# A ring of four transposed inputs in the second mixer, and a last normalisation with its statistics on ScalarE

## What is computed

```python
def _s5_mixer(u, lam_re, lam_im, log_step, b_re, b_im, c_re, c_im, d_skip, w_glu, b_glu):
    ...
    for direction, reverse in ((0, False), (1, True)):
        ...
        bu = jnp.einsum('blgi,gpi->blgp', ugc, b_bar)
        _, states = lax.associative_scan(
            _diag_recurrence, (jnp.broadcast_to(lam_bar, bu.shape), bu), axis=1, reverse=reverse)
        ...
        y = y + jnp.real(jnp.einsum('blgp,gip->blgi', states, c_out))
    y = jax.nn.gelu(y.reshape(bsz, seqlen, S5_WIDTH))
    ...

def _layer_norm(x32, g, b):
    mu = jnp.mean(x32, axis=-1, keepdims=True)
    xc = x32 - mu
    var = jnp.mean(xc * xc, axis=-1, keepdims=True)
    return xc * lax.rsqrt(var + LN_EPS) * g.astype(jnp.float32) + b.astype(jnp.float32)
```

## Time and profile before

| | us |
|---|---|
| median of 3 runs | 3703.0 |
| lowest, highest | 3700.46, 3708.77 |
| the profiled execution | 3708.02 |
| its span, first to last instruction | 3706.2 |

### The profile page before, as it was taken

One profiled execution on the slowest core, in us unless ns is written; L12 is line 12 of the kernel. 1 busy time (PEld: TensorE's weight loads), 2 busy tenths in 40 slices (PEclk: granted clock), 3 DMA queues, 4 the chain that ended last, 5 costly groups with the idle time before them and its releaser, 6 DMA issues. The chain is left out here.

```text
span 3706.2 us, 33835 instructions
## 1 busy us (share of the span) xinstructions
PE 3153.6 (85%) x10424; PEld 1648.4 (44%) x10425; DVE 1432.8 (39%) x2033; ACT 540.3 (15%) x1058; POOL 1210.2 (33%) x1202
## 2 busy tenths in 40 slices
PE   7999999956787467759999928999999999999940
PEld 3555555532555344525555523444444444444420
DVE  2835423413788545513333361222122221222238
ACT  1112222211232100011111101101101101011012
POOL 0116766712666300002222202223222232222329
PEclk9999999977989777879999969999999999999975
DMA  5122232235222364262222124344454354442235
GB/s 238 74 76 80 99 118 94 82 137 211 66 82 89 94 183 145 77 239 91 97 97 91 53 119 151 102 136 125 130 163 126 113 154 152 117 121 45 56 95 206
DMA packets 131695, 437.62 MB, mean 118 GB/s; under 512 B 16884, under 2 KB 45300, under 8 KB 122644
## 3 DMA queue, kind: packets, MB, share of 16 engines
q1 hardware_dynamic: 86488, 291.18, 22.5%
q0 software_dynamic: 24752, 81.35, 9.2%
q10 hardware_dynamic: 20368, 63.94, 4.5%
HBM read 300.03 MB, written 136.38 MB: 118 GB/s over the span
## 5 line engine op out<-in xcount | busy, mean ns | idle before, releaser
L2008 PE MATMUL bank<-wg,exp_ht 128*128 x1008 | 455.0, 594 | 15.4 <-DVE exp_ht L2091 15.4
L2026 PE MATMUL bank<-wd,exp_hid_t 128*128 x1008 | 442.9, 592 | 0.9 <-ACT exp_hid_t L2062 0.9
L2008 PE MATMUL bank<-wu,exp_ht 128*128 x1008 | 442.9, 592 | 0.0
L1967 POOL DMA_INDIRECT x<-exp_out,exp_rows x63 | 102.6, 1629 | 870.0 <-DVE exp_out L2112 826.1
L2112 DVE TENSOR_TENSOR exp_out<-bank,exp_gates 128x512 f32<-128x512 f32 x126 | 81.2, 686 | 778.1 <-PE bank L2026 778.1
L1550 PE MATMUL bank<-mix_wo,mix_yt 128*128 128x512 f32 x768 | 342.4, 600 | 19.0 <-issue 11.5
L571 PE MATMUL bank<-x_t,w_in 128*128 128x512 f32 x768 | 336.0, 596 | 5.4 <-DVE x_t L481 5.4
L571 PE MATMUL bank<-w_in,x_t 128*128 128x264 f32 (+1 forms) x1152 | 339.6, 455 | 0.0
L2026 PEld LDWEIGHTS bank<-wd,exp_hid_t 128*128 128x128 f32 x1008 | 191.4, 190 | 241.6 <-issue 241.6
L2008 PEld LDWEIGHTS bank<-wu,exp_ht 128*128 128x128 f32 x1008 | 191.5, 190 | 241.1 <-issue 241.1
L2008 PEld LDWEIGHTS bank<-wg,exp_ht 128*128 128x128 f32 x1008 | 188.0, 192 | 227.5 <-issue 227.5
(11 more groups left out here) (350 smaller groups left out, 3830.2 us busy)
## 6 DMA issues: line engine op xcount, KB each, us to landing
wg<-in_w_gate SPq DMA_DIRECT2D x16, 2048.0 KB, 7.9
wu<-in_w_up SPq DMA_DIRECT2D x16, 2048.0 KB, 9.2
wd<-in_w_down SPq DMA_DIRECT2D x16, 2048.0 KB, 9.2
x_t<-in_x_t SPq DMA_DIRECT2D x6, 2048.0 KB, 9.2
mix_xt<-in_x SPq DMA_DIRECT2D x6, 2048.0 KB
x<-mix_v ACTq DMA_DIRECT2D x24, 512.0 KB, 2.6
h<-mix_h ACTq DMA_DIRECT2D x24, 512.0 KB, 2.7
com_v<-x SPq DMA_DIRECT2D x24, 512.0 KB, 3.9
```

Source lines behind the costliest of these rows:

```text
L1967: pool.indirect_dma_start(out=y_dram, out_offset=bass.IndirectOffsetOnAxis(ap=rows[:, j:j + 1], axis=0), in_=out[:, j, :], in_offset=None, ...
L2008: mul = pe.matmul(bank[:, :], ht[:, j, k, :], flat(of[:, bass.ds(e % 2, 1), k * DE:(k + 1) * DE]), start=k == 0, stop=k == KT - 1)
L2026: mul = pe.matmul(bank[:, :], hid_t[:, j, k, :], flat(wd[:, bass.ds(e % 2, 1), k * D + q * WIDE:k * D + (q + 1) * WIDE]), start=k == 0, st ...
```

## The change

In `s5_mixer`, `ut` gets four buffers (RING = 4). `turn_u(m)` waits for `y_mm` to reach m-3 instead of m-1, VectorE transposes pairs 0 and 1 first and then pair m+2 ahead of rotate(m). All else in that stage stays as it is.

`combine` is rewritten with six buffers. SyncE loads the first two tiles ahead of `ln_g` and `ln_b`. ScalarE sums each tile (Copy with an accumulated output), VectorE makes the negative mean of it (`centre`, 128x1), ScalarE sums the squares of the centred tile (Square with a bias and an accumulated output), GpSimd makes the reciprocal deviation in two 128x1 operations. VectorE then computes (v - mean) * `ln_g` (`scale`) and that times the reciprocal deviation plus `ln_b` (`shift`), each as one scalar-tensor-tensor operation. ScalarE issues the stores, three tiles behind its sums. In the diff the removed lines of `combine` are left out; they stand above.

```diff
@@ -1197,7 +1197,7 @@
 
     TC = T5 * CH5
     Q = (T5 + 1) * CH5
-    SLOTS = 3
+    SLOTS, RING = 3, 4
     GROUP = 32
     CG = C_ALL // GROUP
     PER = 20
@@ -1207,7 +1207,7 @@
         us = sb("us", [P, CG, HALF, 2, SSD])
         w, e = sb("w", [P, SLOTS, 2, HALF, 2, P]), sb("e", [P, SLOTS, 2, 2, Q])
         turn, toe = sb("turn", [P, SLOTS, 2, 2, C_ALL + 2]), sb("toe", [P, SLOTS, 2, HALF, TC])
-        ut = sb("ut", [P, 2, 2, HALF, C_ALL])
+        ut = sb("ut", [P, RING, 2, HALF, C_ALL])
         m1, m2, x = (sb(n, [P, 2, 2, C_ALL]) for n in ("m1", "m2", "x"))
         z, st = sb("z", [P, 2, 2, C_ALL]), sb("st", [P, 2, 2, 2, C_ALL])
         ys, yp = sb("ys", [C_S, T5, SSD]), sb("yp", [C_P, T5, SSD])
@@ -1251,9 +1251,9 @@
             @block.vector
             def _(dve):
                 def turn_u(m):
-                    j = m % 2
-                    if m >= 2:
-                        dve.wait_ge(y_mm, m - 1)
+                    j = m % RING
+                    if m >= RING:
+                        dve.wait_ge(y_mm, m - RING + 1)
                     for g in range(2):
                         at = (m * 2 + g) * CH5
                         dve.transpose(ut[:, j, g].rearrange("p k (a c) -> p a k c", c=GROUP),
@@ -1299,10 +1299,11 @@
                 dve.memset(z[:], 0.0).then_inc(cleared, 1)
                 dve.wait_ge(u_here, 128)
                 turn_u(0)
+                turn_u(1)
                 dve.wait_ge(cleared, 1)
                 for m in range(PAIRS):
-                    if m + 1 < PAIRS:
-                        turn_u(m + 1)
+                    if m + 2 < PAIRS:
+                        turn_u(m + 2)
                     rotate(m)
 
             @block.tensor
@@ -1318,7 +1319,7 @@
                             for k in range(HALF):
                                 for g in range(2):
                                     mul = pe.matmul(sums[j][d][g * N5:(g + 1) * N5, r * C_ALL:(r + 1) * C_ALL],
-                                                    w[:, s, r, k, d, g * N5:(g + 1) * N5], ut[:, j, g, k, :],
+                                                    w[:, s, r, k, d, g * N5:(g + 1) * N5], ut[:, m % RING, g, k, :],
                                                     start=k == 0, stop=k == HALF - 1)
                     mul.then_inc(states_mm, 1)
 
@@ -1332,7 +1333,7 @@
                         at, c = segments[n]
                         for k in range(HALF):
                             for g in range(2):
-                                pe.matmul(to[n][g], ut[:, j, g, k, at:at + c], toe[:, s, g, k, :], start=k == 0, stop=False)
+                                pe.matmul(to[n][g], ut[:, m % RING, g, k, at:at + c], toe[:, s, g, k, :], start=k == 0, stop=False)
                         if n == 0:
                             pe.wait_ge(e_here[s], loads(m))
                             pe.wait_ge(rotated, (m + 1) * PER)
@@ -2135,101 +2136,107 @@
 
 def combine(nc, C, S, y_dram, ln_g_row, ln_b_row, out_sample, out_prompt):
 
...
+    RING = 6
     with ExitStack() as ctx:
         sb = lambda n, s: ctx.enter_context(nc.sbuf_tensor("com_" + n, s, F32))
         ln_g, ln_b = sb("ln_g", [P, D]), sb("ln_b", [P, D])
...
+        v, y, unused = sb("v", [P, RING, D]), sb("y", [P, RING, D]), sb("unused", [P, 2, D])
+        total, minus, square, root = (sb(n, [P, RING]) for n in ("total", "minus", "square", "root"))
+        g_here, summed, centred, squared, rooted, scaled, shifted = (
+            S(n) for n in ("g_here", "summed", "centred", "squared", "rooted", "scaled", "shifted"))
         v_here, stored = ([S(f"{n}{r}") for r in range(RING)] for n in ("v_here", "stored"))
...
+        uses = lambda n: (n // RING + 1) * 16
+        one = lambda a, n: a[:, n % RING:n % RING + 1]
         with nc.Block() as block:
             @block.sync
             def _(sp):
...
                 for n in range(NT):
                     r = n % RING
                     if n >= RING:
...
+                        sp.wait_ge(scaled, n - RING + 1)
+                        sp.wait_ge(squared, n - RING + 1)
                     sp.dma_start(v[:, r, :], y_dram[n * P:(n + 1) * P, :]).then_inc(v_here[r], 16)
+                    if n == 1:
+                        sp.dma_start(ln_g[:], ln_g_row.to_broadcast([P, D])).then_inc(g_here, 16)
+                        sp.dma_start(ln_b[:], ln_b_row.to_broadcast([P, D])).then_inc(g_here, 16)
                 for r in range(RING):
...
+                    sp.wait_ge(stored[r], NT // RING * 16)
 
             @block.scalar
             def _(act):
...
+                def total_of(n):
+                    act.wait_ge(v_here[n % RING], uses(n))
+                    if n:
+                        act.wait_ge(summed, n)
                     if n >= RING:
...
+                        act.wait_ge(centred, n - RING + 1)
+                    act.activation(unused[:, 0, :], v[:, n % RING, :], ACT.Copy, accum_out=one(total, n)).then_inc(summed, 1)
+
+                def squares_of(n):
+                    act.wait_ge(centred, n + 1)
+                    if n:
+                        act.wait_ge(squared, n)
+                    if n >= RING:
+                        act.wait_ge(rooted, (n - RING) * 2 + 1)
+                    act.activation(unused[:, 1, :], v[:, n % RING, :], ACT.Square, bias=one(minus, n), accum_out=one(square, n)).then_inc(squared, 1)
 
                 def store(n):
...
                     act.wait_ge(shifted, n + 1)
                     to = out_sample[0, n * P:(n + 1) * P, :] if n < NT_SAMPLE else out_prompt[0, (n - NT_SAMPLE) * P:(n - NT_SAMPLE + 1) * P, :]
...
+                    act.dma_start(to, y[:, n % RING, :]).then_inc(stored[n % RING], 16)
+
+                total_of(0)
                 for n in range(NT):
...
+                    if n + 1 < NT:
+                        total_of(n + 1)
+                    squares_of(n)
                     if n >= 3:
                         store(n - 3)
                 for n in range(NT - 3, NT):
                     store(n)
+
+            @block.gpsimd
+            def _(pool):
+                for n in range(NT):
+                    pool.wait_ge(squared, n + 1)
+                    if n >= RING:
+                        pool.wait_ge(shifted, n - RING + 1)
+                    pool.tensor_scalar(one(root, n), one(square, n), 1.0 / D, EPS, ALU.mult, ALU.add).then_inc(rooted, 1)
+                    pool.wait_ge(rooted, n * 2 + 1)
+                    pool.tensor_tensor(one(root, n), one(root, n), C.minus_half[:], ALU.pow).then_inc(rooted, 1)
+
+            @block.vector
+            def _(dve):
+                def centre(n):
+                    dve.wait_ge(summed, n + 1)
+                    if n >= RING:
+                        dve.wait_ge(squared, n - RING + 1)
+                    dve.tensor_scalar(one(minus, n), one(total, n), -1.0 / D, None, ALU.mult).then_inc(centred, 1)
+
+                def scale(n):
+                    r = n % RING
+                    dve.wait_ge(centred, n + 1)
+                    if n >= RING:
+                        dve.wait_ge(stored[r], uses(n) - 16)
+                    dve.scalar_tensor_tensor(out=y[:, r, :], in0=v[:, r, :], scalar=one(minus, n), in1=ln_g[:],
+                                             op0=ALU.add, op1=ALU.mult).then_inc(scaled, 1)
+
+                def shift(n):
+                    r = n % RING
+                    dve.wait_ge(rooted, n * 2 + 2)
+                    dve.wait_ge(scaled, n + 1)
+                    dve.scalar_tensor_tensor(out=y[:, r, :], in0=y[:, r, :], scalar=one(root, n), in1=ln_b[:],
+                                             op0=ALU.mult, op1=ALU.add).then_inc(shifted, 1)
+
+                centre(0)
+                dve.wait_ge(g_here, 32)
+                for n in range(NT):
+                    if n + 1 < NT:
+                        centre(n + 1)
+                    scale(n)
+                    if n:
+                        shift(n - 1)
+                shift(NT - 1)
     S.clear()
```

More of the change, by code:

```diff
@@ L2136, in combine @@
 def combine(nc, C, S, y_dram, ln_g_row, ln_b_row, out_sample, out_prompt):
-    RING = 4
-    TURNS = NT // RING
+    RING = 6
     with ExitStack() as ctx:
@@ L2151, in _ @@
             def _(sp):
-                sp.dma_start(ln_g[:], ln_g_row.to_broadcast([P, D])).then_inc(g_here, 16)
-                sp.dma_start(ln_b[:], ln_b_row.to_broadcast([P, D])).then_inc(g_here, 16)
                 for n in range(NT):
@@ L2159, in _ @@
                 for r in range(RING):
[L2160 to L2166, removed]
-                    for q in range(2):
-                        dve.bn_stats(stats[:, r, q, :], v[:, r, q * WIDE:(q + 1) * WIDE]).then_inc(counted, 1)
-                    dve.wait_ge(counted, n * 2 + 2)
-                    dve.bn_aggr(mean[:, r, :], flat(stats[:, r:r + 1].rearrange("p a b c -> p (a b) c"))).then_inc(meant, 1)
-                def scale(n):
-                    r = n % RING
```

(45 more changed lines are left out.)

9 lines of the change are left out of this document (removed).

## The result

The changed kernel takes 3556.45 us (median of 4 runs, 3552.65 to 3561.33) against 3704.69 us for the kernel before (4 runs, 3700.46 to 3708.77; the three known ahead of the prediction and one more). The ratio is 0.9601, with a 95% interval of 0.9584 to 0.9617: 148 us less, where 139 were forecast.

The account below looks back on a forecast made before the run. Bounds: VectorE and TensorE taking turns in the second mixer, GpSimd's 4.48 us per tile in the last normalisation. 3708.0 - 102 - 36.7 = 3569.3, forecast as 3564 us because the median lies 5.0 lower; range 3550 to 3606.

Parts of the forecast that it names:

- The stall of the transposes goes: Second mixer: transposes for pair m+2 wait for output m-2 instead of m-1, so VectorE's 7.87 us stall goes.
- TensorE becomes the bound, at 9.45 us: Second mixer: TensorE's 9.45 us a pair exceeds VectorE's 9.13 by 0.3 us and sets the pace.
- The clock comes back in full: Second mixer: TensorE's granted clock, 0.80 over a pair before, returns to full level; 43 us of the gain hang on it.
- The beginning costs nothing: Second mixer's start: two more transposes (2 x 1.04 us) ahead of rotation 0 run beside TensorE's first states, at no cost.
- 1.7 us for one short wait in the middle: Middle of the second mixer: deduction of 1.7 us because the 3 MB store of the first half shares engines with loads.
- A tile of 3.0 us: Last normalisation: 3.0 us for each of 24 tiles, ends 2.82 and 3.42; stage gains 36.7 us, bounds 26.6 and 41.
- Start at `ln_g`'s landing: Last normalisation: VectorE's first scaling needs `ln_g` and starts at about 3592.0 again, though ScalarE can start up to 3.5 us earlier.
- A: Rival, second mixer: TensorE still falls to 1.2 GHz in each pair, mixer gains 60 us, total 3606; chance 0.09.
- D: Rival, second mixer: TensorE stays at 1.2 GHz throughout, 20.1 us a pair, total 3716, slower; chance 0.02.
- B: Rival, last normalisation: VectorE-GpSimd exchange becomes a chain of 4.5 us a tile, gaining nothing; total 3601, chance 0.08.
- C: Rival, second mixer: rotation waits for TensorE's states, pair stays at 17 us, only the normalisation gains; total 3666, chance 0.03.
- DMA as a possible bound: Last normalisation: DMA needs 2.69 us a tile; if ScalarE waits for loads of `v`, DMA was the bound.

Follow-up runs that it names:

- e9: Changed kernel without the second scalar-tensor-tensor operation of each tile and with each store of the last normalisation writing half the columns; one run, 3544.28 us.
- e8: Changed kernel without GpSimd's two small operations per tile in the last normalisation, the sum of squares standing in for the reciprocal deviation; one run, 3553.76 us.
- e7: Changed kernel without the second scalar-tensor-tensor operation of each tile in the last normalisation; one run, 3551.86 us.
- e11: Changed kernel with ScalarE's sum reading its scale of one from a 128x1 operand; sum 1135 ns against 1044, tile 2.46 us.
- e6: Changed kernel with each store of the last normalisation writing only the first 512 of 1024 columns; one run, 3554.24 us.

## Why the prediction was right, point by point

- **The stall of the transposes goes: right**, and for the reason given; the ring of three shows that it is the output waited for, not the lead.
- **TensorE becomes the bound, at 9.45 us: right**, 9.49 measured, and VectorE has 0.34 us a pair to spare where the sum had 0.3.
- **The clock comes back in full: right**, 1.00. Its size was put at 43 us for the changed kernel; given back alone in the kernel before, it is 37.
- **The beginning costs nothing: off by 1.4 us.** Output 0 ends 55.6 us behind the first load (1275.70 to 1331.26), before it was 54.2. TensorE's granted clock over 1310 to 1330 is 0.72 instead of 0.78, and its second group of states takes 5.39 us where it took 4.42.
- **1.7 us for one short wait in the middle: not there.** The stretch from 1407.00 shows the DMA full, at 338 GB/s, and TensorE busy throughout. This and the point above cancel, which is luck; the -101.9 for a forecast of -102 is closer than the terms are.
- **A tile of 3.0 us: too long, 2.45 measured**, and this is all of what the forecast missed (24 x 0.55 = 13 us, less about 1 for the start and the end; in spans 151.5 us were gained for a forecast of 138.7, in medians 148 for 139). It lay below the low end of 2.82, and the stage's 48.7 us beyond the 41 that were given as its bound; the total stays in the range because the mixer came out near the middle of its own. Three terms were mis-sized. For ScalarE I took the 1.24 us of an operation with two 128x1 operands, twice, and added the store's 0.34; measured are 1.04 and 1.14 (L2173 and L2181 above), the accumulator reads and the store's issue hide, and the need is 2.17 (e9). For VectorE I allowed 0 to 0.79 us for GpSimd; it is 0, as e8 shows. What remained was VectorE's own 2.45, below its 2.63 in the sum: the long operations start 1.20 us apart where 1.225 was taken, and the tiny one adds 0.06 where 0.18 was. For the DMA the sum had 2.69; full, it needs 2.48 (e7). The Trainium skill, page "ScalarE: Activation LUTs", section "What ACT_TABLE_LOAD costs", gives 186 ns + 0.833 ns per element for a pass without a 128x1 operand and about 93 ns more for each; an estimate by it is 1.04 and 1.13 us for these two passes. The trace agrees, and e11 shows the step of one operand by itself.
- **The Trainium skill's rule** on the page "SBUF — State Buffer", section "SBUF: two separate sides", by which a tile would have taken 3.42 us: the trace agrees for GpSimd, whose operations grew from 192 ns (shortest) to 814 ns (median) and from 578 to 1470 ns beside VectorE's; it does not for VectorE, whose rows do not change when GpSimd's two small operations are gone. The measurement decides.
- **Start at `ln_g`'s landing: right in kind.** VectorE's first scaling came 8.2 us behind the first load, forecast 7.5; what ended its wait was the load of `ln_b`, the last of the four.
- **Rivals.** A (clock falls in each pair) and D (low level throughout) are refuted by the clock of 1.00, B (a chain through the tile) by e7 and e9, in which the tile shortens with the work, C (rotation waits for states) by the wait of 0.34 us.
- **DMA as a possible bound:** its share is 0.99 and yet it is not what bounds these 24 tiles; e6 tells it apart, and e7 shows it only 0.03 us a tile from being the bound. Landing of stores went from 4.1 to 7.0 us and was covered by the ring of six.
- **Slips in the working that changed nothing.** The loads of a pair add up to 1956 KB, 2.00 million bytes and not 2.04, which is 212 GB/s at 9.45 us; the pair from 1388.00 shows 212. The mixer's bound at VectorE's 9.13 us comes to -108 and not -109. Of the 21.93 us of VectorE's idling ahead of the last normalisation, only 7.5 lie behind the stage's first load.

## What to carry to other kernels

When an engine's idle time is one wait behind another engine's last step, work out which earlier step the wait would have to name for both to run through; the number of buffers minus the lead gives it, and a lead alone gives nothing. A pause of TensorE costs twice where the granted clock drops behind it, so the price of a pause is read from the matmuls that follow it too. Take durations from an operation with the same function and the same number of 128x1 operands, and count the distance between starts, not the recorded length. Where the DMA stands right beside the busiest engine, a shorter program for that engine gains only until the buffers ahead are used up, and a mean over a short stage hides that; compare the pace of its first tiles with that of its last.

## What was not expected of the hardware

- With matmuls of zeros between two groups the granted clock was 1.00 in a pair of 14.1 us, where it had been 0.80 in one of 17.0.
- GpSimd's 128x1 operations between VectorE's scalar-tensor-tensor operations cost VectorE nothing that can be seen (1.27 us with and without), while GpSimd's became 0.6 and 0.9 us longer themselves. In the kernel before, where GpSimd's operation was 128x1024, VectorE's multiplication had a mean of 2.85 us.
- Loads and stores together ran at 400 GB/s over 45 us and at 416 GB/s when VectorE had less to do, at a share of 0.99 to 1.02 of the 16 engines; the loads of `u` filled them (1.04) at 202 GB/s.
